# Loading four of an expert's 48 weight units as 112 + 8 + 8 rows instead of 128

## The chip, the cores and the metric

The kernel runs on one core of one Trainium2 chip. The time is device microseconds of one execution; before the change it is 1390.87 us as the median of three runs (1390.38 to 1391.24). TensorE (PE) multiplies, VectorE (DVE), ScalarE (ACT) and GpSimd (POOL) do the rest, SyncE (SP) does nothing but issue loads, and 16 transfer engines carry what is loaded.

## The reference

The reference is a trunk of two layers over 272 tokens (16 meta tokens and 256 frames) of width 1024, in float32. Each layer has an attention part and a feed-forward part; the first feed-forward part is dense, the second has eight experts of which each token uses two:

```python
def moe_swiglu(h, router_w, w_gate, w_up, w_down):
    logits = (h @ router_w).astype(jnp.float32)
    top_val, top_idx = lax.top_k(logits, TOP_K)
    gates = jax.nn.softmax(top_val, axis=-1)
    ...
    for e in range(N_EXPERTS):
        out = out + gate_dense[..., e:e + 1] * swiglu(h, w_gate[e], w_up[e], w_down[e])
    return out
```

with `swiglu(h, ...) = (silu(h @ w_gate) * (h @ w_up)) @ w_down` and an inner width of 3584. The expert weights alone are 352 MB, and every one of them is used once.

## The kernel before

**Stages.** Attention, dense feed-forward, attention, and then the expert stage, from about 522 us of the trace to its end. All weights lie in one HBM tensor, `stream`, cut into units of 128 rows (one row to a partition of the on-chip memory) by up to 2048 columns.

**An expert.** `moe_order` (lines 122 to 131) cuts it into 48 units: 32 of kind "w" (gate and up weights, 128 x 1792, 896 KB), then 16 of kind "d" (down weights; in each of four groups three of 128 x 2048, 1024 KB, and one of 128 x 1024, 512 KB). Every expert takes up to 96 tokens in three tiles of 32, one expert (the second in order of work) in two. For a "w" unit PE runs 12 matmuls (24 records of the trace), for a "d" unit 12 or 24; the second expert needs two thirds of that.

**The ring.** Unit m goes to slot m % 16 of `MOE_SLOTS` = 16 slots. Some slots lie in `moe_ring`, some in `parts_ring`, one in `sq`; those are three names for memory that earlier stages used. Each slot has its own semaphore, `slot_in[m % 16]`. A load adds 16 to it when it has landed, and PE waits for the count in `arrival` (line 990) before it reads the unit.

**Who sets the order.** SP runs `load_expert` (line 429 on) once per expert. For each unit it waits until PE is done with the unit 16 earlier (`w_used`), then issues one load of all 128 rows:

```python
sp.wait_ge(w_used, it * EXPERT_UNITS + (MOE_SPLIT + m - MOE_SLOTS + 1))
sp.dma_start(moe_unit(m), stream[e * EXPERT_UNITS + (MOE_AT + m), :, 0:moe_cols(key)]).then_inc(
    slot_in[m % MOE_SLOTS], 16)
```

The first expert is written out; the other seven run in a loop, so that SP's counts come out of registers. PE writes out the first six experts, and has register counts for the last two. POOL gathers the tokens of the next expert and adds up the results of the last one with DMAs of its own, which share the 16 transfer engines with the weights.

Of the kernel before, what the change touches and what calls it, by code (L numbers as in the profile page):

```python
# [41 lines left out]
P = 128  # L42
# [22 lines left out]
SLOTS = 6  # L65
HSLOTS = 3
MOE_SLOTS = SLOTS + 2 * HSLOTS + 4
# [8 lines left out]
MOE_AT = 2 * ATTN_UNITS + FFN_UNITS  # L76
# [3 lines left out]
EXPERT_UNITS = FF_GROUPS * (DK + (FF_TILES + 1) // 2)  # L80
# [39 lines left out]
def ffn_order():  # L120

    order = [("g", 0), ("u", 0)]
    for c in range(1, CHUNKS):
        order += [("g", c), ("u", c), ("d", c - 1)]
    return order + [("d", CHUNKS - 1)]


def moe_order():

    def up(g):  # L130
        return [("w", g, k) for k in range(DK)]

    def down(g):
        return [("d", g, i) for i in range((FF_TILES + 1) // 2)]

    return up(0) + up(1) + up(2) + up(3) + down(0) + down(1) + down(2) + down(3)


FFN_ORDER = ffn_order()
FFN_POS = {key: n for n, key in enumerate(FFN_ORDER)}  # L140
MOE_ORDER = moe_order()
MOE_POS = {key: m for m, key in enumerate(MOE_ORDER)}
# [2 lines left out]
def moe_cols(key):  # L145

    return 8 * FQ if key[0] == "w" else D * min(2, FF_TILES - 2 * key[2])


def is_direct(n):  # L150

    return (n - (ATTN1_AT if n >= ATTN1_AT else 0)) in DIRECT
# [14 lines left out]
def build(nc, stream, h0, gains, router_w, fnorm, consts, out):  # L167
    with ExitStack() as ctx:
        def sb(name, shape, dt=F32):
            return ctx.enter_context(nc.sbuf_tensor(name, shape, dt))  # L170

        def sem(name):
            return ctx.enter_context(nc.semaphore(name))
# [41 lines left out]
        key, least, smallest = sb("key", [P, EXPERTS]), sb("least", [P, EXPERTS]), sb("smallest", [P, 4])  # L215
# [75 lines left out]
        slot_in = [sem(f"slot_in{i}") for i in range(MOE_SLOTS)]  # L291
# [65 lines left out]
        def moe_unit(m):  # L357

            return moe_slots[m % MOE_SLOTS][:, 0:moe_cols(MOE_ORDER[m])]

        def moe_arrivals(m):

            return 16 * ((MOE_AT // SLOTS if m % MOE_SLOTS < SLOTS else 0) + m // MOE_SLOTS + 1)

        def arrived(eng, unit):

# [2 lines left out]
        def split(eng, unit):  # L369

            n = SPLIT_OF[unit]
            eng.wait_ge(split_lo, n + 1)
            return w_hi[:, n % HSLOTS, :], w_lo[:, n % HSLOTS, :]
# [8 lines left out]
        def o_(name, layer):  # L382
            return layer * N_OUTS + OUTS.index(name)
# [23 lines left out]
        @block.sync  # L407
        def _(sp):
            def load(n, cols=UNIT):
                if n >= SLOTS:  # L410
                    old = n - SLOTS
                    if is_direct(old):
                        sp.wait_ge(direct_used, DIRECT_OF[old] + 1)
                    else:
                        sp.wait_ge(split_lo, SPLIT_OF[old] + 1)
                sp.dma_start(ring[:, n % SLOTS, 0:cols], stream[n, :, 0:cols]).then_inc(slot_in[n % SLOTS], 16)

            for u, c, i, end in PIECES:
                sp.dma_start(ring[:, u, c], stream[u, :, c]).then_inc(slot_in[u] if end else first_in[i], 16)
            load(2)  # L420
            load(3)
            sp.dma_start(c_sb[:, :], consts).then_inc(const_in, 16)
            sp.dma_start(rw_sb[:, :, :], router_w).then_inc(rw_in, 16)
            for n in range(4, MOE_AT):
                b = n - ATTN1_AT if n >= ATTN1_AT else n
                load(n, used_cols.get(b, UNIT) if b < ATTN_UNITS else UNIT)
                if n == ATTN1_AT + U_T2:
                    sp.wait_ge(rope_done, 2 * N_ROPES)
                    sp.dma_start(gain_row, fnorm[:, 1, :]).then_inc(gain_in, 16)

            def load_expert(it, e):
                for m, key in enumerate(MOE_ORDER):
                    if m < SLOTS:
                        old = MOE_AT - SLOTS + m
                        if is_direct(old):
                            sp.wait_ge(direct_used, DIRECT_OF[old] + 1)
                        else:
                            sp.wait_ge(split_lo, SPLIT_OF[old] + 1)
                    elif m == 6:
                        sp.wait_ge(out_done, o_("g3", 1) + 1)  # L440
                    elif m in (7, 8):
                        sp.wait_ge(w_used, MOE_SPLIT - 2)
                    elif m in (9, 10):
                        sp.wait_ge(w_used, MOE_SPLIT - 1)
                    elif m == 11:
                        sp.wait_ge(mla_read, 2)
                    elif m in (12, 13, 14):
                        sp.wait_ge(w_used, MOE_SPLIT)
                    elif m == 15:
                        sp.wait_ge(tok_square, 4)  # L450
                    sp.wait_ge(w_used, it * EXPERT_UNITS + (MOE_SPLIT + m - MOE_SLOTS + 1))  # L451
                    sp.dma_start(moe_unit(m), stream[e * EXPERT_UNITS + (MOE_AT + m), :, 0:moe_cols(key)]).then_inc(  # L452
                        slot_in[m % MOE_SLOTS], 16)

            def load_others(r):
                with sp.Fori(1, EXPERTS) as n:
                    load_expert(r * EXPERTS + n, sp.value_load(order_sb[0:1, n, :], min_val=1, max_val=EXPERTS - 1))

            load_expert(0, 0)
            sp.wait_ge(order_ready, 1)  # L460
            load_others(0)
            sp.wait_ge(rounds_ready, 1)
            rounds = sp.value_load(rounds_sb[0:1, 0:1], min_val=1, max_val=ROUNDS)
            with sp.If(rounds > 1):
                with sp.Fori(1, rounds) as r:
                    load_expert(r * EXPERTS, 0)
                    load_others(r)
            with sp.Else():
                sp.nop()

            sp.wait_ge(res_ready, 1)
            sp.dma_start(out[0:P, :], res[:, 0, :]).then_inc(out_stored, 16)
            sp.wait_ge(res_ready, 2)
            sp.dma_start(out[P:2 * P, 0:512], res[:, 1, 0:512]).then_inc(out_stored, 16)
            sp.wait_ge(out_stored, 48)
# [138 lines left out]
        def _(pe):  # L614
# [310 lines left out]
            def dense():  # L925
                def gate_up(c):
                    for j, kind in enumerate("gu"):
                        w = [x.rearrange("p (k c) -> p k c", k=DK) for x in split(pe, DENSE_AT + FFN_POS[kind, c])]
                        first = c == 0 and j == 0
# [16 lines left out]
                def down(c):  # L946
                    w = [x.rearrange("p (f n) -> p f n", f=2) for x in split(pe, DENSE_AT + FFN_POS["d", c])]
                    pe.wait_ge(a_ready, c + 1)
                    if c == 0:
                        pe.wait_ge(std_ready, 2)  # L950
                    for d in range(DK):
                        if c or d >= 4:
                            pe.wait_ge(h_added, 8 + c * DK + d - 3)
                        for f in range(2):
                            mm3(bank[4 + d % 4][:, 0:L], [x[:, f, d * P:(d + 1) * P] for x in w],
                                [ad_hi[c % 2][:, f, :], ad_lo[c % 2][:, f, :]], f == 0, f == 1, d_done if f == 1 else None)
                    used_up.append((w_used, 1))
# [30 lines left out]
            def expert(it, last=False, tiles=range(TILES_OF), first=False):  # L988

                def arrival(key):  # L990

                    m = MOE_POS[key]
                    pe.wait_ge(slot_in[m % MOE_SLOTS], it * (16 * EXPERT_UNITS // MOE_SLOTS) + moe_arrivals(m))
                    return moe_unit(m)

                def both(s):
# [97 lines left out]
        def _(act):  # L1094
# [182 lines left out]
            def dense():  # L1277
                for m, (kind, c) in enumerate(FFN_ORDER):
                    n = SPLIT_OF[DENSE_AT] + m + HSLOTS
                    if kind == "u":  # L1280
                        act.wait_ge(af_ready, c + 1)
                        A(ad_hi[c % 2], a_dense, ACT.Copy).then_inc(a_hi_ready, 1)
                    if m < FFN_UNITS - 1:
                        high(n)
                    if kind == "g":
                        act.wait_ge(g_scaled, c + 1)
                        A(sil_dense, sil_dense, ACT.Silu).then_inc(silu_done, 1)
# [120 lines left out]
        def _(dve):  # L1408
# [242 lines left out]
            def dense():  # L1651
# [6 lines left out]

                for m, (kind, c) in enumerate(FFN_ORDER):
                    n = SPLIT_OF[DENSE_AT] + m + HSLOTS  # L1660
# [294 lines left out]
```

## Time and profile before

| | |
|---|---|
| median of three runs | 1390.87 us |
| the profiled execution, its own time | 1388.64 us |
| its span in the trace | 1386.8 us |
| granted TensorE clock, mean | 0.998 |
| PE busy | 1354.0 us, 98% |
| DVE, ACT, POOL busy | 469.0, 342.9, 84.2 us |
| moved from HBM | 438.20 MB |

The page's slices are a fortieth of the span each, 34.7 us. "Busy" for PE is time with a matmul under way. The DMA share of a stretch is the mean busy share of the 16 transfer engines; it can read a little over 1, since neighbouring packets of an engine overlap. A stretch's GB/s counts all queues.

### The profile page before, as it was taken

The page shows a single profiled execution, that of the slowest core. Times are in us where ns is not written, and L with a number is a line of the kernel's source. Part 1 is how long each engine was busy: PE and PEld are TensorE (multiplying, and loading weights), DVE is VectorE, ACT ScalarE, POOL GpSimd, SP SyncE. Part 2 cuts the span into 40 slices and gives each one's busy share as a digit, 9 for nine tenths or more (in the row PEclk, how much of TensorE's full clock was granted, in tenths as well). Part 3 has the DMA queues.
Part 4 walks back from the last instruction along what each step waited for, and adds up shares of the span by engine and source line. Part 5 has one row for each costly group of instructions (what it writes and reads, how often), then busy time and mean ns, then how long its engine had stood idle before and what let it go on. Part 6 is the DMA issues. An engine that isn't in the chain of part 4 may idle for free.

```text
span 1386.8 us, 34063 instructions
## 1 busy us (share of the span) xinstructions
PE 1354.0 (98%) x15034; PEld 866.5 (62%) x15034; DVE 469.0 (34%) x822; ACT 342.9 (25%) x594; POOL 84.2 (6%) x113
## 2 busy tenths in 40 slices
PE   9999999999999999999879999999999999999997
PEld 8889999999998894464333353363353354344344
DVE  7777777766797651101101101100100100110011
ACT  7666533333386641001000000000000000000011
POOL 0000000000000015001010010001001001001000
PEclk9999999999999999999999999999999999999999
DMA  9316644444433189999999999999999999999993
GB/s 362 112 58 244 228 166 162 174 183 183 183 134 138 62 325 412 417 418 408 418 414 416 419 417 410 419 417 412 419 417 409 418 417 410 417 415 406 419 414 137
DMA packets 74249, 443.98 MB, mean 320 GB/s; under 512 B 10116, under 2 KB 12224, under 8 KB 52992
## 3 DMA queue, kind: packets, MB, share of 16 engines
q1 hardware_dynamic: 67824, 433.04, 77.3%
q0 software_dynamic: 5424, 7.45, 2.0%
q8 instruction: 118, 1.93, 0.6%
q10 hardware_dynamic: 864, 1.40, 0.3%
q14 instruction: 19, 0.16, 0.0%
HBM read 438.20 MB, written 5.93 MB: 320 GB/s over the span
## 4 chain that ended last, share of the span: by engine, by line
PE 66%; SPq 19%; DMA 8%; DVE 2%; issue 2%; ACT 2%; ACTq 0%; DVEq 0%
PE bank L626 64%; SPq L452 19%; DMA moe_ring<-stream 6%; DMA parts_ring<-stream 2%; DMA hT<-h 1%; DVE w_lo L1425 1%; PE bank L630 0%; PE bank L724 0%; SPq L451 0%; DVE nmx L1510 0%; ACT scratch L1180 0%; PE bank L730 0%; ACT w_hi L1102 0%; ACT scratch L1179 0%; PE bank L1069 0%
## 5 line engine op out<-in xcount | busy, mean ns | idle before, releaser
L626 PE MATMUL bank<-parts,w_hi 128*128 128x272 f32 (+1 forms) x2240 | 427.5, 289 | 2.0 <-DVE parts L1439 1.7
L626 PE MATMUL bank<-moe_ring,hT 128*32 128x448 f32 x4416 | 425.3, 539 | 3.6 <-DMA moe_ring<-stream 2.9
L626 PEld LDWEIGHTS bank<-parts,w_hi 128*128 128x128 f32 x2240 | 351.9, 188 | 5.6 <-issue 4.2
L626 PE MATMUL bank<-parts,w_lo 128*128 128x272 f32 (+1 forms) x1120 | 321.4, 287 | 0.0
L626 PEld LDWEIGHTS bank<-moe_ring,hT 128*32 128x32 f32 x4416 | 149.3, 110 | 268.0 <-issue 242.0
L1777 DVE SCALAR_TENSOR_TENSOR hT<-bank,slot_norm,scratch 128x224 f32<-128x224 f32 x96 | 40.8, 425 | 727.3 <-ACT scratch L1332 727.2
L626 PE MATMUL bank<-moe_ring,scratch 128*32 128x256 f32 x4048 | 225.0, 379 | 9.3 <-DMA moe_ring<-stream 9.2
L626 PEld LDWEIGHTS bank<-parts,w_lo 128*128 128x128 f32 x1120 | 211.0, 188 | 0.2
L626 PEld LDWEIGHTS bank<-moe_ring,scratch 128*32 128x32 f32 x4048 | 133.9, 110 | 98.8 <-DMA moe_ring<-stream 16.1
L1332 ACT ACTIVATE scratch<-bank,norm_now 128x224 f32<-128x224 f32 x96 | 42.4, 447 | 513.6 <-PE bank L626 513.0
L1425 DVE TENSOR_TENSOR w_lo<-ring,w_hi 128x2048 fp32r<-128x2048 f32 x68 | 154.6, 2287 | 32.2 <-ACT w_hi L1102 32.1
L1102 ACT ACTIVATE w_hi<-ring 128x2048 fp32r<-128x2048 f32 x68 | 129.6, 1912 | 90.1 <-PE bank L626 90.0
L626 PE MATMUL bank<-parts_ring,hT 128*32 128x448 f32 x1104 | 112.9, 539 | 1.6 <-DMA parts_ring<-stream 1.6
L626 PEld LDWEIGHTS bank<-parts_ring,hT 128*32 128x32 f32 x1104 | 37.0, 110 | 69.0 <-issue 59.4
L1342 ACT ACTIVATE scratch<-bank,slot_gate 128x256 f32<-128x256 f32 x21 | 9.3, 474 | 246.3 <-PE bank L626 246.3
L1657 DVE TENSOR_TENSOR hT<-hT,bank 128x272 f32<-128x272 f32 x112 | 48.6, 435 | 20.8 <-PE bank L626 19.8
L626 PE MATMUL bank<-parts_ring,scratch 128*32 128x256 f32 x920 | 54.2, 379 | 1.1 <-DMA parts_ring<-stream 1.1
L576 POOL DMA_INDIRECT scratch<-hn_rows,row_of x24 | 25.0, 1040 | 448.5 <-DVE hT L1789 442.8
L585 POOL DMA_INDIRECT acc_rows<-scratch,row_of x21 | 33.3, 1587 | 213.4 <-ACT scratch L1342 209.1
L626 PEld LDWEIGHTS bank<-parts_ring,scratch 128*32 128x32 f32 x920 | 30.5, 110 | 20.7 <-DMA parts_ring<-stream 2.3
L1780 DVE STREAM_TRANSPOSE scratch<-hT 128x224 f32<-128x224 f32 x96 | 39.5, 411 | 3.3
L626 PE MATMUL bank<-sq,hT 128*32 128x448 f32 x368 | 37.6, 539 | 0.5 <-DMA sq<-stream 0.5
(227 smaller groups left out, 626.6 us busy)
## 6 DMA issues: line engine op xcount, KB each, us to landing
moe_ring<-stream SPq DMA_DIRECT2D x192, 896.0 KB, 24.1
moe_ring<-stream SPq DMA_DIRECT2D x80, 1024.0 KB, 25.3
ring<-stream SPq DMA_DIRECT2D x68, 1024.0 KB, 5.0
parts_ring<-stream SPq DMA_DIRECT2D x48, 896.0 KB, 23.8
parts_ring<-stream SPq DMA_DIRECT2D x16, 1024.0 KB, 24.9
sq<-stream SPq DMA_DIRECT2D x16, 896.0 KB, 23.6
moe_ring<-stream SPq DMA_DIRECT2D x16, 512.0 KB, 24.7
parts_ring<-stream SPq DMA_DIRECT2D x8, 512.0 KB, 25.1
```

What stands on the lines that cost most here:

```text
L452: sp.dma_start(moe_unit(m), stream[e * EXPERT_UNITS + (MOE_AT + m), :, 0:moe_cols(key)]).then_inc(slot_in[m % MOE_SLOTS], 16)
L576: pool.indirect_dma_start(out=x_rows[:, s, :], out_offset=None, in_=hn_quarters, in_offset=bass.IndirectOffsetOnAxis(ap=row_of[:, s, n:n + ...
L585: pool.indirect_dma_start(out=acc_quarters, out_offset=bass.IndirectOffsetOnAxis(ap=row_of[:, s, n:n + 1], axis=0), in_=ye[:, s, :], in_of ...
L626: return release(nc.tensor.matmul(dst, lhsT, rhs, start=start, stop=stop), inc, count)
L1102: A(w_hi[:, n % HSLOTS, :], slot(UNIT_OF[n]), ACT.Copy).then_inc(split_hi, 1)
L1332: A(sil_moe[:, s, :], bank[UP_BANKS[g][s]][:, 0:FQ], ACT.Silu, scale=norm_now[:, s:s + 1]).then_inc(e_silu, 1)
L1342: A(ye[:, s, :], bank[DOWN_BANKS[s]][:, 0:256], ACT.Copy, scale=slot_gate[:, it, s:s + 1]).then_inc(ye_ready, 1)
L1425: V.tensor_tensor(w_lo[:, n % HSLOTS, :], slot(UNIT_OF[n]), w_hi[:, n % HSLOTS, :].bitcast(F32), ALU.subtract).then_inc(split_lo, 1)
L1657: V.tensor_tensor(hT[:, d, :], hT[:, d, :], bank[4 + d % 4][:, 0:L], ALU.add).then_inc(h_added, 1)
L1777: V.scalar_tensor_tensor(out=a_moe[:, s, :], in0=bank[UP_BANKS[g][s]][:, FQ:2 * FQ], scalar=slot_norm[:, it, s:s + 1], in1=sil_moe[:, s, : ...
L1780: V.transpose(ht[:, g, s, :], a_moe[:, s, :]).then_inc(ht_ready, 1)
```

## The change

Units 5, 17, 29 and 41 of each expert ("w", "w", "w" and a "d" unit of 2048 columns) are loaded in three transfers: rows 0 to 111, 112 to 119 and 120 to 127. The rows, the memory they go to and the bytes are the same. All three add 16 to the slot's semaphore, so PE's count for such a slot is the sum of what its loads add.

```diff
+LEANING = (5, 17, 29, 41)
+LEAN_CUTS = (0, 112, 120, 128)
...
+        def moe_loads(m):
+
+            return len(LEAN_CUTS) - 1 if m in LEANING else 1
+
         def moe_arrivals(m):
 
-            return 16 * ((MOE_AT // SLOTS if m % MOE_SLOTS < SLOTS else 0) + m // MOE_SLOTS + 1)
+            each = [x for x in range(EXPERT_UNITS) if x % MOE_SLOTS == m % MOE_SLOTS]
+            count = (MOE_AT // SLOTS if m % MOE_SLOTS < SLOTS else 0) + sum(moe_loads(x) for x in each if x <= m)
+            return 16 * count, 16 * sum(moe_loads(x) for x in each)
...
-                    sp.dma_start(moe_unit(m), stream[e * EXPERT_UNITS + (MOE_AT + m), :, 0:moe_cols(key)]).then_inc(
-                        slot_in[m % MOE_SLOTS], 16)
+                    cuts = LEAN_CUTS if m in LEANING else (0, P)
+                    for a, b in zip(cuts, cuts[1:]):
+                        sp.dma_start(moe_unit(m)[a:b, :], stream[e * EXPERT_UNITS + (MOE_AT + m), a:b, 0:moe_cols(key)]).then_inc(
+                            slot_in[m % MOE_SLOTS], 16)
...
-                    pe.wait_ge(slot_in[m % MOE_SLOTS], it * (16 * EXPERT_UNITS // MOE_SLOTS) + moe_arrivals(m))
+                    count, each = moe_arrivals(m)
+                    pe.wait_ge(slot_in[m % MOE_SLOTS], it * each + count)
```

Rows that go 8 to an engine in a transfer of 128 go 7 to an engine in one of 112 spread over 16 engines; a transfer of 8 rows gives one row each to eight engines.

On SP, where the first expert's loads begin (`ring` is the memory of the stages before; each row is a run of equal loads), before:

```order
L416 DMA ring<-stream 128x2048 x4
L452 DMA moe_ring<-stream 128x1792 x6
L452 DMA parts_ring<-stream 128x1792
L452 DMA moe_ring<-stream 128x1792 x4
L452 DMA parts_ring<-stream 128x1792
L452 DMA moe_ring<-stream 128x1792 x2
```

and now:

```order
L424 DMA ring<-stream 128x2048 x4
L462 DMA moe_ring<-stream 128x1792 x5
L462 DMA moe_ring<-stream 112x1792
L462 DMA moe_ring<-stream 8x1792 x2
L462 DMA parts_ring<-stream 128x1792
L462 DMA moe_ring<-stream 128x1792 x4
```

The sixth load has become three, directly behind one another; nothing else changes its place.

On PE, where the loop over the last experts but one begins (`hT` holds the gathered tokens), before:

```order
L1088 ISA
L993 ISA
L626 MATMUL bank<-moe_ring,hT 32x448 x72
L993 REGISTER_ALU
L626 MATMUL bank<-parts_ring,hT 32x448 x12
```

and now:

```order
L1099 ISA
L1004 ISA
L636 MATMUL bank<-moe_ring,hT 32x448 x12
L1004 ISA
L636 MATMUL bank<-moe_ring,hT 32x448 x48
L1004 REGISTER_ALU
L636 MATMUL bank<-moe_ring,hT 32x448 x12
L1004 REGISTER_ALU
L636 MATMUL bank<-parts_ring,hT 32x448 x12
```

Slots no longer share one count per expert, so PE works out more register values between the same matmuls: 32 rows more in all (2642 after 2610).

## Rows read from the trace of the kernel before

**Rows 1.** The page's head, and its slices of the span.

```profile
span 1386.8 us, 34063 instructions
PE 1354.0 (98%) x15034; PEld 866.5 (62%) x15034; DVE 469.0 (34%) x822; ACT 342.9 (25%) x594; POOL 84.2 (6%) x113
...
GB/s 362 112 58 244 228 166 162 174 183 183 183 134 138 62 325 412 417 418 408 418 414 416 419 417 410 419 417 412 419 417 409 418 417 410 417 415 406 419 414 137
```

**Rows 2.** Busy time by stretch, one expert each from the second on.

```profile
core 0: us, PE busy (x) PEld busy (x) DVE busy (x) ACT busy (x) POOL busy (x), PEclk, DMA share, GB/s
630.40:717.80 87.40, 75.85 (x975) 32.89 (x964) 10.38 (x27) 6.41 (x18) 7.92 (x6) 1.00 1.02 414
717.80:827.90 110.10, 108.81 (x1438) 46.82 (x1436) 10.42 (x27) 6.75 (x18) 7.85 (x6) 1.00 1.02 416
827.90:936.40 108.50, 108.50 (x1447) 46.65 (x1440) 10.41 (x27) 6.89 (x18) 7.86 (x6) 1.00 1.02 415
936.40:1045.60 109.20, 108.75 (x1448) 46.34 (x1440) 10.41 (x27) 6.88 (x17) 7.88 (x6) 1.00 1.02 416
1045.60:1154.20 108.60, 108.60 (x1448) 46.67 (x1442) 10.42 (x27) 6.93 (x18) 7.84 (x6) 1.00 1.02 415
1154.20:1263.60 109.40, 108.65 (x1448) 46.63 (x1440) 11.93 (x33) 6.92 (x18) 7.92 (x6) 1.00 1.02 414
1263.60:1377.00 113.40, 112.08 (x1503) 49.24 (x1492) 11.99 (x26) 9.12 (x21) 5.57 (x4) 1.00 0.87 355
```

**Rows 3.** The DMA issues of SP's line 452: duration of an issue in ns.

```profile
L452 SPq DMA_DIRECT2D moe_ring<-stream x288: 327/1652/7537, 481.4 to 1343.2; - x144
L452 SPq MOVE moe_ring<-stream x252: 29/29/38, 597.6 to 1343.2; - x126
```

**Rows 4.** From the same view: time from issue to landing.

```profile
DMA to landing us min/median/max: 4.6/24.3/29.8
```

**Rows 5.** DMA issues by line, KB each, median us to landing.

```profile
moe_ring<-stream SPq DMA_DIRECT2D x192, 896.0 KB, 24.1
...
slot_sb<-slot_rows POOLq DMA_DIRECT2D x4, 28.1 KB, 5.6
```

**Rows 6.** PE in order of time, 1290 to 1300 us.

```profile
1290.60 2.46 PE L626 MATMUL bank<-parts_ring,hT 128*32 128x448 f32 x24 [1.12 <-DMA parts_ring<-stream]
1292.88 4.69 PE L626 MATMUL bank<-moe_ring,hT 128*32 128x448 f32 x48
1297.39 2.44 PE L626 MATMUL bank<-parts_ring,hT 128*32 128x448 f32 x24
```

**Rows 7.** Stretches about four 32-row loads of POOL (columns as in rows 2).

```profile
536.00:543.00 7.00, 7.00 (x80) 2.98 (x76) 2.35 (x6) 1.34 (x3) 2.32 (x4) 1.00 1.02 420
543.00:547.00 4.00, 4.00 (x48) 1.69 (x44) 0.00 (x0) 0.00 (x0) 0.00 (x0) 1.00 1.03 371
547.00:552.00 5.00, 5.00 (x60) 2.09 (x55) 0.00 (x0) 0.00 (x0) 3.17 (x8) 1.00 1.01 415
```

**Rows 8.** POOL after those loads.

```profile
547.66 0.28 POOL L560 CAST row_f<-slot_sb 128x75 f32<-128x75 int32 x1 [5.56 <-DMA slot_sb<-slot_rows]
```

**Rows 9.** Stretches at the head of the stage (columns as in rows 2).

```profile
500.00:510.00 10.00, 10.00 (x89) 10.00 (x88) 4.48 (x7) 1.90 (x5) 0.69 (x2) 1.00 0.71 262
510.00:520.00 10.00, 9.27 (x78) 8.69 (x77) 4.87 (x21) 4.33 (x12) 3.53 (x11) 1.00 1.01 410
```

**Rows 10.** DMA queues from 480 to 1377 us: packets, MB, share of 16 engines.

```profile
q1 hardware_dynamic: 55440, 353.39, 95.7%
q0 software_dynamic: 5120, 6.37, 2.7%
q8 instruction: 90, 1.47, 0.7%
```

## What the change was predicted to do

> **What bounds the kernel now.** I read the page's head first, to see where the loads run flat out: from the sixteenth slice on the stream stays at 406 to 419 GB/s, and before that it is mostly far below [rows 1]. The change touches only expert loads, so the question is what bounds that stretch. Cut by expert, the DMA share is 1.02 in every window from 630 to 1264 us: no transfer engine has time to spare there [rows 2]. PE is busy 108.5 us of 108.5 in one expert and 75.85 of 87.40 in the second one, which has only two tiles. PE's idle time is the window less its busy time: 11.55, 1.29, 0, 0.45, 0, 0.75 and 1.32 us, 15.4 us in all. That is all that a better stream could give back.
>
> PE and the stream are nearly equal. PE takes 2.28 us for a "w" unit (1290.60 to 1292.88) and 2.26 when nothing waits (4.51 for two) [rows 6]. A "w" unit is 896 KB, 917.5 kB, which at 415 GB/s is 2.21 us. PE's own pace thus has 0.05 us a unit over the stream, and a late landing stops PE as in the 1.12 us of [rows 6]. From issue to landing it takes 24 us as the median, about eleven units, and an issue itself takes 1.65 us against 0.33 at best [rows 3, 4]: SP stands in a full queue. So more issues cost SP nothing while that queue is full, and what counts is when the slowest of the 16 engines has its share done.
>
> **The change part by part.** In a full transfer each engine carries 8 rows, so a row of a "w" unit takes 2.21 / 8 = 0.275 us of an engine.
>
> *The row moved.* In a leaned unit one half of the engines has 7 rows and the other 9. If the half with 7 is the one that lands last, it is 0.275 us earlier per leaned unit. Of the 32 leaned units, the first lies about 500 to 510 us, where the share is 0.71 and the queue runs empty [rows 9]; what is saved there is lost again. Behind it the queue stays full, so 31 count: -8.5 us for that half, and +8.5 us for the other.
>
> *The cost of the form.* The trace has no transfer of 8 or of 112 rows. The nearest are POOL's four loads of 32 rows, 28.1 KB each [rows 5], which end before 547.66 us [rows 8]. While they run, the total falls from 420 to 371 GB/s, though the share is 1.03 [rows 7]: the engines are busy and move less. In these 4 us that is 196 kB less in total; the narrow loads are 115 kB of what is moved, so the weights lose 311 kB for 115 kB of narrow load, 2.7 for one. The two pieces of 8 rows are 16 x 7168 bytes = 115 kB as well. At 2.7 for one they take 311 kB of the stream instead of their own 115: 196 kB at 415 GB/s, 0.47 us a leaned unit. The bounds: nothing, if the narrow loads are slow only because their rows are short; and, from above, all 128 rows at 2.7 for one, 1.7 x 2.21 = 3.8 us. I take 0.47, since the 8-row pieces are what resembles that row; the 112-row piece I take as free. The net is 0.47 - 0.275 = +0.2 us for the half that lands last, and 31 x 0.2 = +6 us; the bounds are -8.5 (cut to -6 by what PE can give back, below) and 31 x 3.5 = +109 us.
>
> *Issues.* 64 more at 0.33 us are 21 us on SP if nothing hid them. SP has 2.2 us a unit and needs 0.33; three issues are 1 us. They are hidden by the full queue: 0.
>
> *Register work.* PE has 32 rows more; the nearest duration is a MOVE of 29 ns on SP [rows 3], 0.9 us if uncovered. PE's sequencer runs ahead of matmuls that are back to back: 0. The wait on 48 instead of 16 ends with the last piece, which is directly behind the others in the queue.
>
> The sum is made on the profiled execution: 1388.64 + 6 = 1394.6 us, of which 1.8 lie outside the span of 1386.8. The runs' median is 2.2 above the profiled time, so 1396.8, say 1397 us.
>
> At this place the Trainium skill weighs against the change. "SBUF — State Buffer", section "Door 1: The DMA port swizzle", says that the 128 partitions share 16 write ports, eight partitions to a port, four neighbours together, and that bandwidth goes by how many ports a transfer reaches. "DMA: Bandwidth & Descriptors", section "Why a DMA increments its semaphore by 16 and not by 1", says that a transfer of 8 rows runs on the eight lowest engines. By the two, eight engines push 8 rows through two ports that others are using. The trace agrees in direction, with its 371 after 420 GB/s, but its rows cannot tell ports from short packets. No view names an engine.
>
> **The rivals.**
>
> *Favourable: the form is free.* For it: rows of 7168 bytes are long, those of the narrow loads were short, and PE does wait for a stream whose mean rate would do. Something must make some engines later than others: instruction packets take 0.7% of 16 engines' 897 us, 100 us [rows 10]. If they all fall on eight engines, those are behind by 100 / 8 = 12.5 us at the end. The half with 7 rows gains 8.5, and the other half, 12.5 ahead, loses 8.5 and ends 4 ahead of where the late one was: 4 us gained at least, 6 if the gap is wider. From PE's side: by 727 us eight units are leaned, 2.2 us off the 11.55 idle, and the later idle 3.8 us go, 6 us. I take -5: 1386 us. Against it: it needs the misfit to be below 0.27 us, 4% of three transfers.
>
> *Pile-up.* Four neighbouring rows of an 8-row piece share one way into memory that passes a row in 0.275 us. The engine that always uses that way gets four strange rows for the one it is spared: +3 x 0.275 = +0.82 us a unit, 31 x 0.82 = +25, 1416 us; and if the 112 rows misfit likewise, up to 1500. It decides once a way carries no more than one engine does, since the share has no slack [rows 2]. Against it: a stream whose halves are many us apart may dodge it. By the page's ports this is the outcome; the trace does not show it.
>
> *The wrong half.* If the engines that take 9 rows are those that land last, then 31 x 0.275 = +8.5 us, 1399 us. Nothing in the rows says which half is late.
>
> *It does nothing.* If the engines' queues take the rows as before, whatever the shape, or gain and cost cancel: 1391 us.
>
> **How the numbers follow.** The forecast (a misfit near the narrow loads' price) has 0.34, favourable 0.33, pile-up 0.17, wrong half 0.06, nothing 0.10. The likeliest is the forecast by a hair, and its own range is 1393 to 1405. Within 0.2% is 2.8 us, about what a measurement of this kernel can tell from no change. Faster 0.34 takes the favourable case and the little of "nothing" that falls there; same 0.12 takes the rest of "nothing" and a forecast whose net comes out near 0; slower 0.54 is what remains. The range leaves out the upper part of the pile-up and the edge of the favourable: 1384 to 1440 us.
>
> **What would show it.** Right: the DMA share stays at 1.02 while GB/s in windows with a leaned unit is lower; an expert takes 0.8 us longer than 108.5 and PE waits for a load in every one. Favourable: GB/s unchanged or up, PE's idle time in the second expert's window falls by about 2 us and the later ones' is gone. Pile-up: an expert takes 3 us or more longer, and loads behind a leaned unit land later too, 27 us or more after issue. The form costs nothing at SP if its issues still have a median near 1.65 us. I am wrong in the net if experts come at 108.3 us with no waits, and wrong about SP if PE waits where SP's queue is short of loads.

## The result, and the profile after

| | before | after |
|---|---|---|
| median of the timed runs | 1390.93 us (4 runs) | 1569.87 us (4 runs, 1565.74 to 1587.72) |
| ratio after / before | | 1.1313, 95% interval 1.1285 to 1.1342 |
| the profiled execution, its own time | 1388.64 us | 1571.56 us |

The kernel is 13% slower. The forecast of 1397 us is wrong, and so is its range, which ended at 1440. The sign and the place were right, and the size was far off: 179 us over 32 leaned units are 5.6 us each, more than the 2.21 us that a whole "w" unit takes on the stream.

The page of the changed kernel, beside [rows 1]: its head, the DMA share and GB/s of the 40 slices (39.2 us each), the weights' queue, and the chain of waits by engine.

```profile
span 1569.7 us, 34255 instructions
PE 1399.4 (89%) x15034; PEld 854.6 (54%) x15034; DVE 469.2 (30%) x822; ACT 342.5 (22%) x594; POOL 84.1 (5%) x113
...
DMA  8334544454335999999999999999999999999993
GB/s 339 130 125 189 203 182 162 162 186 157 120 125 200 377 366 369 327 340 348 354 329 312 314 330 343 333 347 327 331 350 349 347 337 353 352 335 359 339 349 115
...
q1 hardware_dynamic: 68336, 433.05, 79.0%
...
PE 39%; SPq 38%; DMA 15%; issue 3%; DVE 2%; ACT 1%; ACTq 0%; DVEq 0%
```

The work is the same (PE has as many matmuls as in [rows 1]), and the engines of the transfers are as full as before. What they move has fallen from 406 to 419 GB/s to 312 to 377. In the chain, SP's full queue and the DMAs together (53%) now stand ahead of PE (39%). Before, the same line of the page read:

```profile
PE 66%; SPq 19%; DMA 8%; DVE 2%; issue 2%; ACT 2%; ACTq 0%; DVEq 0%
```

The windows by expert, columns as in [rows 2]:

```profile
631.50:757.00 125.50, 86.98 (x975) 31.58 (x965) 10.39 (x27) 6.42 (x18) 7.92 (x6) 0.93 1.02 347
757.00:901.80 144.80, 114.76 (x1440) 44.03 (x1436) 10.42 (x27) 6.74 (x18) 7.84 (x6) 0.99 1.02 320
901.80:1038.20 136.40, 114.32 (x1448) 43.40 (x1440) 10.42 (x27) 6.88 (x17) 7.86 (x6) 1.00 1.00 333
1038.20:1171.00 132.80, 114.62 (x1448) 44.82 (x1443) 10.41 (x27) 6.90 (x17) 7.87 (x6) 0.99 1.00 339
1171.00:1300.40 129.40, 113.15 (x1448) 45.27 (x1444) 10.42 (x27) 6.90 (x17) 7.83 (x6) 1.00 1.00 349
1300.40:1429.80 129.40, 112.70 (x1448) 44.27 (x1444) 11.93 (x33) 6.91 (x18) 7.92 (x6) 1.00 0.99 343
1429.80:1560.00 130.20, 119.15 (x1504) 48.25 (x1492) 12.01 (x26) 9.14 (x21) 5.57 (x4) 0.96 0.85 298
```

An expert of three tiles takes 129 to 145 us in place of 109. In the third to seventh expert of [rows 2] PE's idle time was 0 to 1.3 us each; it is now 16 to 30 us (144.80 less 114.76 is 30.0). The stage went from being bound by PE and the stream together to being bound by the stream alone. In the second expert's window PE's granted clock is 0.93, but PE stands idle for 38.5 us of it, so the clock is not what makes it longer. Every expert from the second on pays, so it is no mishap at one place. The first pays almost nothing yet: it takes 109.0 us (522.5 to 631.5) for 107.9, though its stream moves 362 GB/s for 415. PE is still fed there from what was loaded ahead, and the bill comes in the second expert, 38 us longer.

The loads into `moe_ring`, first what SP does, then who waits for them and how long from issue to landing, beside [rows 3] and [rows 4]; and PE's waits over the expert stage (us in all, times, longest):

```profile
L462 SPq DMA_DIRECT2D moe_ring<-stream x352: 242/1752/10242, 481.5 to 1525.8; - x176
...
DMA to landing us min/median/max: 10.2/28.5/35.5
```

```profile
PE bank L636 <- DMA moe_ring<-stream: 127.6, 123, 2.8
...
PEld bank L636 <- DMA moe_ring<-stream: 246.0, 200, 3.3
```

Before, PEld waited 38.7 us in 67 waits for `moe_ring`, and PE 12.0 us in 16. The longest of these waits has hardly grown, 3.3 us after 2.6: there is no long stop at the leaned units, PE is short of weights by a little at very many units. An issue has a median of 1.75 us for 1.65, so SP stands in a full queue as before, and the three issues are not what costs. A load lands 28.5 us after its issue instead of 24.3. The queue holds the same work, and the engines take longer for it.

That can be seen on single packets, which the trace keeps with their sizes and times (no view prints them). A row of a "w" unit is one packet of 7168 bytes. Before, its mean in the stage is 276 ns (half of them within 272 and 278); after, between 700 and 1500 us, it is 336 ns, a quarter take 360 or more, and one in twenty 536 or more, which is about twice 272. The rise, 1.22 times, is that from 340 to 415 GB/s. So it is not a few slow packets in the small pieces: the packets of the whole loads are longer too (those of the "d" units' 8192 bytes take 381 ns for 315), as would be seen if two engines took turns at one place.

The engines also drift apart in another way. Of one whole load of slot 15 these are the landings of its 16 shares, in us behind the first (one engine each):

```
before, at 1099.5 us:  0.6 3.5 3.5 4.0 4.1 4.2 4.4 | 11.8 12.4 12.7 13.5 13.6 13.8 14.1 16.0
after, at 1103.0 us:   0.2 0.2 0.3 0.3 1.0 1.0 1.4 2.4 2.8 5.0 6.5 6.6 13.8 17.9 20.7
```

Before there are two halves of eight. The means of the first eight and the last eight shares are 1 us apart at 531 us, 3 at 640, 10 at 1100 and 14 at 1317. This is the lean that the favourable rival supposed. After, the two halves are gone, and three engines are 14 to 21 us behind all others. A load is complete with its last share, so PE waits for the slowest engine.

### The profile page after: what moved, and what is told of

It is laid out like the page before. It is cut to its first block, busy times and chain, and to the rows that moved or that the text cites. A ratio compares the mean times of both kernels' runs of the same rounds, so it can differ in the third digit from the quotient of the medians.

```text
span 1569.7 us, 34255 instructions
## 1 busy us (share of the span) xinstructions
PE 1399.4 (89%) x15034; PEld 854.6 (54%) x15034; DVE 469.2 (30%) x822; ACT 342.5 (22%) x594; POOL 84.1 (5%) x113
## 4 chain that ended last, share of the span: by engine, by line
PE 39%; SPq 38%; DMA 15%; issue 3%; DVE 2%; ACT 1%; ACTq 0%; DVEq 0%
PE bank L636 38%; SPq L462 38%; DMA moe_ring<-stream 13%; DMA parts_ring<-stream 2%; DMA hT<-h 1%; DVE w_lo L1436 1%; SPq L459 0%; PE bank L640 0%; PE bank L734 0%; DVE nmx L1521 0%; ACT scratch L1191 0%; PE bank L740 0%; ACT w_hi L1113 0%; ACT scratch L1190 0%; PE bank L1080 0%
## 5 line engine op out<-in xcount | busy, mean ns | idle before, releaser
L636 PE MATMUL bank<-moe_ring,hT 128*32 128x448 f32 x4416 | 447.2, 548 | 82.5 <-DMA moe_ring<-stream 81.5
L636 PEld LDWEIGHTS bank<-moe_ring,hT 128*32 128x32 f32 x4416 | 140.4, 110 | 381.9 <-issue 202.0
L636 PE MATMUL bank<-moe_ring,scratch 128*32 128x256 f32 x4048 | 236.9, 385 | 46.5 <-DMA moe_ring<-stream 46.1
L636 PEld LDWEIGHTS bank<-parts_ring,scratch 128*32 128x32 f32 x920 | 30.6, 112 | 29.1 <-DMA parts_ring<-stream 11.8
```

The source lines that it names most:

```text
L636: return release(nc.tensor.matmul(dst, lhsT, rhs, start=start, stop=stop), inc, count)
```

## The experiments

**Theories.** *Places* (1): engines and the rows that they write no longer fit together, so that two engines at a time want the same way into the on-chip memory. *Fixed costs* (2): each further transfer costs the engines something whatever its form. *The small pieces* (3): the 8-row transfers are slow by themselves, as the prediction held. *The lean* (4): one row more on the eight engines that are late. And within the first, whether it is the place that is written or the place that is read.

In the kernels of the expert stage `moe_cuts(m)` gives the rows and columns of unit m's transfers; a "-" line is the change itself, written in that form. The loads of units not named stay whole, and PE's counts follow the number of transfers.

### e1: three transfers of all 128 rows each

```diff
-            return [(slice(a, b), slice(0, cols)) for a, b in ((0, 112), (112, 120), (120, P))]
+            return [(slice(0, P), slice(a, b)) for a, b in ((0, cols - 256), (cols - 256, cols - 128), (cols - 128, cols))]
```

> The four units of each expert in three transfers again, but cut by columns: 128 rows of all but 256 columns, then twice 128 rows of 128 columns (512 bytes a row). Every transfer keeps 8 rows to an engine. Theory 1 (ways into memory: the time comes from rows that an engine writes where another engine usually writes): no such row here, so 1391 to 1397 us, with GB/s of an expert window back at 410 or more. Rival (number of transfers, or the sum on one semaphore, costs): as the changed kernel, near 1570 us, since there are as many transfers.

Measured: 1393.74 us (1393.35 to 1394.46), ratio 1.0037 (1.0022 to 1.0051). The page's GB/s slices:

```profile
GB/s 362 109 58 245 230 166 166 166 179 182 182 151 134 61 328 408 417 414 407 416 408 417 417 414 408 417 415 409 416 415 407 416 401 410 410 410 406 417 405 158
```

The same number of transfers and issues in the same units, cut by columns, costs 5.0 us instead of 179, and the stream keeps its 401 to 417 GB/s. So the number of transfers, SP's issues and PE's register work are not the cause. The 5.0 us are 0.08 us for each of the 64 further transfers. They agree with the packets: a row is now 6144 + 512 + 512 bytes, 238 + 28 + 28 = 294 ns in place of 276; 18 ns by 8 rows by 32 units is 4.6 us.

### e2 and e3: two pieces, 112 + 16 and 64 + 64 rows

```diff
-            return [(slice(a, b), slice(0, cols)) for a, b in ((0, 112), (112, 120), (120, P))]
+            return [(slice(a, b), slice(0, cols)) for a, b in ((0, 112), (112, P))]   # e2
+            return [(slice(a, b), slice(0, cols)) for a, b in ((0, 64), (64, P))]     # e3
```

> The same units as 112 + 16 rows: two transfers, both over 16 engines, 7 and 1 rows to each, so no engine carries more than another. Theory 1 (ways into memory): the 112 rows stay where they were and are most of the bytes; between 1480 and 1600 us. Rival 1 (it is the lean: nine rows on eight engines): back to 1391 to 1400 us. Rival 2 (the eight-row pieces pile up on few ways and the 112 rows are harmless): 1420 to 1480, since 16 rows still come to the same places, by 16 engines.

> The same units as 64 + 64 rows: two transfers over 16 engines, 4 rows of each to an engine, no lean, no small piece. Theory 1 (ways into memory): all 16 engines write one half's eight ways at once, so a unit needs at least twice 2.21 us, and the other engines' units suffer too: 32 x 2.2 = 70 us or more over 1391, 1460 to 1600 us. Rival (small pieces or the lean): 1391 to 1397 us.

Measured: e2 1562.62 and 1592.67 us, too far apart for a ratio. No engine carries more than another there, and even the lower one is 174 us above the kernel before. e3 1573.99 us (1565.79 and 1582.19), ratio 1.1334 (1.1265 to 1.1402). The 100 us from 1000 on of e3 (columns as in rows 2):

```profile
1000.00:1100.00 100.00, 83.46 (x1114) 34.86 (x1108) 4.71 (x12) 4.22 (x11) 4.77 (x3) 1.00 0.99 344
```

With 64 + 64 there is no piece of 8 rows and nothing of 112, and the two pieces are alike, yet the price is the same within the runs' spread. So neither 8-row pieces nor a lean is needed for it: theory 3 is out as the cause, and theory 4 is at most a side matter. What the three row cuts share is that a unit's rows go out in a transfer that does not cover all 128.

### e4: one leaned unit per expert

```diff
-LEANING = (5, 17, 29, 41)
+LEANING = (17,)
```

> Only unit 17 of each expert in 112 + 8 + 8 rows, the other three whole. If every leaned unit has a price of its own (179 us / 32 = 5.6 us): 8 x 5.6 = 45 us less what PE's pace hides, 1420 to 1436 us. If the price is one of a state that the stream falls into and stays in: well over 1436. If one leaned unit is hidden by the queue and only several in a row hurt: under 1400.

Measured: 1443.24 us (1442.36 and 1444.12), ratio 1.0392 (1.0371 to 1.0413): 54.5 us for eight leaned units, 6.8 each. Its slices:

```profile
GB/s 361 119 59 236 234 175 176 176 173 174 121 124 136 174 380 408 417 389 385 417 406 358 418 409 336 418 409 329 419 415 329 412 416 356 377 409 386 358 409 109
```

That is above the 1420 to 1436 that I expected for a price of 5.6 us a unit. The stream falls to 329 to 358 once per expert and is back at 409 to 419 between. So a misfit heals within less than an expert, and each leaned unit pays its own price. Shorter stretches show how (columns as in rows 2, the first three around one leaned unit each):

```profile
646.00:656.00 10.00, 10.00 (x113) 4.07 (x106) 1.02 (x3) 1.20 (x3) 0.00 (x0) 1.00 1.00 237
868.00:888.00 20.00, 13.34 (x140) 3.68 (x132) 2.35 (x6) 1.34 (x3) 0.00 (x0) 1.00 1.02 269
1096.00:1124.00 28.00, 20.18 (x208) 5.69 (x204) 2.35 (x6) 1.34 (x3) 0.00 (x0) 1.00 1.02 305
1124.00:1136.00 12.00, 12.00 (x135) 4.13 (x130) 0.00 (x0) 0.00 (x0) 0.00 (x0) 1.00 1.01 418
```

One leaned unit, 2.2 us of stream by itself, slows the stream for 10, 20 and 28 us. Against 415 GB/s that is 4.3, 7.0 and 7.4 us lost. In the third a packet of 7168 bytes takes 380 ns in the mean, directly behind it (the fourth line) 277. The disturbance grows as the engines drift apart: the first and the last share of a load of slot 15 land 5 us apart at 643 us of e4, 14 at 866 and 21 at 1093, so it is 5 to 7 us longer than that distance each time. The further apart the engines are, the longer some of them are at the leaned unit while others are not. That this is the reason is my inference. In the changed kernel the next leaned unit comes twelve units or 26.5 us later, late in the stage before such a disturbance would be over. That may be part of why its price per unit is lower (5.6 us).

### e7: another place read, the same place written

```diff
+SHIFT = 36
...
-            return [(slice(a, b), slice(0, cols)) for a, b in ((0, 112), (112, 120), (120, P))]
+            return [(slice(0, P), slice(0, cols))]
...
+                        if m in LEANING:
+                            at = (MOE_AT + m) * P + SHIFT
+                            source = stream.rearrange("n p c -> (n p) c")[at:at + P, cols]
```

> Units 5, 17, 29 and 41 in one transfer of 128 rows as before, but its source begins 36 rows further on in HBM (and is the first expert's unit for every expert, so these weights are others). Each engine writes where it always writes and reads rows that another engine usually reads. Theory 1 (the price is paid where rows are written, in the on-chip memory): as before the change, 1387 to 1392 us. Rival (it is paid where rows are read, in HBM): tens of us more, up to 1570.

Measured: 1389.88 us (10 runs, 1389.49 to 1390.36), ratio 1.000 (0.9991 to 1.001).

```profile
1000.00:1100.00 100.00, 99.84 (x1347) 65.16 (x1343) 8.04 (x21) 5.56 (x14) 7.83 (x6) 1.00 1.02 415
```

In the same four units the rows read from HBM begin 36 rows further on, and what is written lies where it did. (They are always those of the first expert's unit, so this kernel leaves out the right weights of four units.) It costs nothing. For a transfer of 128 rows the place that is read does not matter, and I leave it out of the explanation.

### e8, e9 and e10: the same small transfer to three sets of places

All units are loaded whole. Behind each "w" unit goes one further transfer of 8 rows by 1 KB, into columns that no "w" unit uses. It has the same bytes and issues in the three kernels and takes the same part in the queue; only the partitions differ.

```diff
+LEANING = tuple(range(32))
...
+            return [(slice(0, P), slice(0, cols)), (slice(0, 32, 4), slice(cols, UNIT))]      # e8: rows 0, 4, .. 28
+            return [(slice(0, P), slice(0, cols)), (slice(64, 96, 4), slice(cols, UNIT))]     # e9: rows 64, 68, .. 92
+            return [(slice(0, P), slice(0, cols)), (slice(112, 120), slice(cols, UNIT))]      # e10: rows 112 to 119
```

> Nothing is split: each of the 32 'w' units is loaded whole, and a second transfer adds 8 rows of 1 KB (rows 0, 4, ..., 28, into columns that the unit leaves free; 256 such transfers). By theory 1 these eight rows go to eight different ways, which the eight engines that carry them use anyway. A row of 1 KB is about 0.04 us of an engine, 10 us in all for those eight engines. If they are the half that is ahead: 1389 to 1393 us. If they are the half that is late: 1398 to 1404.

> As the one with rows 0, 4, ..., 28, but with rows 64, 68, ..., 92: the same eight engines carry the same bytes, now to the eight ways that the other eight engines use. By theory 1 the other half is held up by what is written there, 0.04 us a unit or 10 us in all, and more if a held-up row costs more than its own length: 1398 to 1420 us, and above the run with the low rows by 8 us or more. Rival (only engines count, not places): the same time as the run with the low rows, within 3 us.

> As the two with every fourth row, but with rows 112 to 119, side by side. By theory 1 four of them share one way, so two ways get 4 x 0.04 = 0.16 us a unit, 256 x 0.16 = 41 us in all on the two engines that always write there: 1415 to 1440 us. Rival (only engines count): as the run with the low rows.

| | rows | us | ratio |
|---|---|---|---|
| e8 | 0, 4, .. 28 | 1407.87 | 1.013 (1.0113 to 1.0147) |
| e9 | 64, 68, .. 92 | 1416.37 | 1.019 (1.0173 to 1.0207) |
| e10 | 112 to 119 | 1420.83 | 1.0227 (1.021 to 1.0244) |

Only the places differ, and e9 is 8.5 us and e10 13.0 us above e8, with no overlap (the runs of each lie within 2 us). Both are where I expected them. 8.5 us over 256 transfers are 0.033 us each. This shows an effect of place on transfers of 8 rows, and in the order that theory 1 gave; but it is small.

My expectation for e8, 1389 to 1404, was missed. I had left out what such a transfer costs of itself: its packet of 1 KB takes 46 ns in the trace, 256 of them 11.8 us on an engine that has no slack. The other packets are longer too, 279.7 ns in e8, 283.4 in e9 and 281.5 in e10 for 276.4 before, which over 860 us is 10, 22 and 16 us. Together that is 22, 34 and 28 us for the 18, 27 and 31 that were lost. It does not explain why e10 is above e9; a mean over 16 engines does not say what the slowest did. Between 1000 and 1100 us the three move 405, 404 and 401 GB/s at a share of 1.00 to 1.01; the kernel before moves 415.

In e8 the two halves of a whole load have merged. At 1150.6 us its shares land at 0.0 0.1 ... 2.1 6.4 7.3 15.8 behind the first. That fits if the eight engines that took the small packets had been the early ones and lost their lead; one engine is 16 us late, and I have no cause for it.

### e5 and e6: only the 112 rows, only the 8-row pieces

From the second expert on (28 units) only a part of the four units is loaded.

```diff
+            return [(slice(0, P), slice(0, cols))] if first else [(slice(0, 112), slice(0, cols))]                        # e5
+            return [(slice(a, b), slice(0, cols)) for a, b in ((0, 64), (64, P))] if first else [(slice(a, b), slice(0, cols)) for a, b in ((112, 120), (120, P))]   # e6
```

> From the second expert on, units 5, 17, 29 and 41 bring only rows 0 to 111 (rows 112 to 127 keep what an earlier unit left there); the first expert's come whole. 28 leaned units, no eight-row piece. If the 112 rows carry the price, as 112 + 16 and 64 + 64 rows suggest: 28 x 4 to 5.6 us, less 28 x 0.28 us for the rows left out, 1490 to 1540 us. If the eight-row pieces carry it: 1383 to 1389.

> The other part alone: from the second expert on, these four units bring only rows 112 to 119 and 120 to 127 in two transfers (the first expert's come as 64 + 64 rows). That leaves out 28 x 1.93 us = 54 us of the stream, far more than the 15.4 us that PE can give back. If the eight-row pieces cost less than about 2 us a unit they are hidden, and the time is 1374 to 1390 us (the first expert's 64 + 64 rows may add up to 20). If they carry most of the 5.6 us: 28 x 3.7 = 103 us more than that, 1480.

Measured: e5 1529.98 us (1526.51 and 1533.45), ratio 1.102 (1.096 to 1.1079); e6 1395.78 us (1392.79 to 1396.16), ratio 1.0048 (1.0028 to 1.0067). Both from 1000 us on, e5 first:

```profile
1000.00:1100.00 100.00, 84.64 (x904) 28.46 (x900) 10.42 (x27) 6.91 (x17) 7.88 (x6) 0.97 1.02 334
```

```profile
1000.00:1100.00 100.00, 100.00 (x1356) 43.90 (x1352) 10.41 (x27) 6.91 (x17) 7.84 (x6) 1.00 1.02 397
```

The 112-row piece alone, with 475 kB less per expert to move, costs 141.6 us, 5.1 per unit. That is nearly the whole. It was the piece that I had taken as free.

In e6 PE has no idle time in this stretch, so what the 8-row pieces cost is hidden there by the 112 rows that are not loaded: 3326 kB an expert, 8.0 us at 415 GB/s, so at most about 2 us for each of four units. They are not free: the share is 1.02 although only 397 GB/s are moved. An estimate from this: 18 GB/s less than 415 over an expert's 109 us are 4.7 us, or 1.2 us for each of the four units. As to the 7.4 us above the kernel before, e6 loses them early. Counted by matmuls, PE is 0.5 us behind the kernel before when that one is at 613 us, 14 us behind at 703 us, and 7 at the end. So they come from the first expert's 64 + 64 rows or the first of the 8-row pieces; which of the two, this run does not say.

### e11 and e12: the price alone, on an idle queue

In the dense feed-forward stage the queue is not full (a whole unit of 1024 KB lands 5.0 us after its issue, in the expert stage 25.3). Twelve of its units of 1024 KB are cut, and the expert stage is left as before.

```diff
+CUT = tuple(range(DENSE_AT + 12, DENSE_AT + 36, 2))
...
-                sp.dma_start(ring[:, n % SLOTS, 0:cols], stream[n, :, 0:cols]).then_inc(slot_in[n % SLOTS], 16)
+                    sp.dma_start(ring[rows, n % SLOTS, c], stream[n, rows, c]).then_inc(slot_in[n % SLOTS], 16)   # e11: rows 0 to 111, 112 to 127; e12: columns 0 to 1791, 1792 to 2047
```

> The expert stage is as before. In the dense stage, where transfers often find an empty queue (a whole unit lands 5.0 us after its issue), twelve units are loaded as 112 + 16 rows. Theory 1: with nobody beside them, the engines of a 112-row transfer (896 KB) collide only with one another; it lands later than the same 896 KB by columns, by 0.5 to 2 us. If the price needs neighbours that are out of step: the same landing within 0.3 us. The whole time within 3 us of before, since this stage does not wait for the loads.

> The same twelve dense units as 128 rows of 1792 columns (896 KB) and 128 rows of 256 columns: the control for the run with 112 + 16 rows. The 896 KB transfers land 4.4 to 4.9 us after issue, a little less than the 5.0 of a whole unit; whole time within 3 us of before.

Measured: 1388.72 and 1389.07 us (8 runs each), ratios 1.0003 (0.9992 to 1.0015) and 1.0005 (0.9993 to 1.0016). The DMA issues of e11 and of e12 (KB each, median us from issue to landing):

```profile
ring<-stream SPq DMA_DIRECT2D x12, 896.0 KB, 6.1
...
ring<-stream SPq DMA_DIRECT2D x12, 128.0 KB, 6.9
```

```profile
ring<-stream SPq DMA_DIRECT2D x12, 896.0 KB, 4.5
...
ring<-stream SPq DMA_DIRECT2D x12, 128.0 KB, 4.6
```

Here the bytes of the pieces are equal. 896 KB as 112 rows land after 6.1 us, as 128 rows of fewer columns after 4.5: the misfit of such a transfer is 1.6 us where it runs beside little but its own small piece. The kernel's time does not show it, since nothing waits for these units. The same form costs 5 to 7 us per unit in the full stream, three to four times as much. There the loads around it are slowed as well, as e4's stretches of 10 to 28 us show.

**What the runs settle.** Cutting by rows costs, cutting by columns almost nothing (e1 against e2, e3); most of it sits in the large piece (e5 against e6); it belongs to each unit (e4) and is paid in longer packets of all loads around it. What they do not settle is why. The place read costs nothing in whole transfers (e7), and the place written matters for 8-row transfers, by 8.5 to 13 us in 256 of them (e8 to e10). No run writes the rows of a large piece to other places or by other engines. So the collision at a way into memory is an inference from these and from packets that take up to twice as long; no view shows such a way. That something else in how a transfer of 64 or 112 rows is dealt out to the engines lengthens the packets is left as a rival.

## Why the prediction was wrong

**The step that failed** is "the cost of the form", and in it the half sentence "the 112-row piece I take as free". The term was +0.47 us a unit, put on the two 8-row pieces. It measures 5.6 + 0.275 = 5.9 us if the row moved brought what I gave it, and e5 shows 5.1 of it in the 112 rows. My reason was that the 8-row pieces resembled the only narrow load in the trace [rows 5, 7]. Likeness of size was the wrong likeness: what the narrow loads showed was busy engines that move less. In those 4 us the weights' own packets of 7168 bytes took 310 ns in the mean, for 274 in the 7 us ahead of them, so the neighbours paid. This held for every transfer of fewer than 128 rows that I ran, and most for the one with seven times the rows of the two small pieces. The term for the small pieces was low as well, 0.47 us for an estimated 1.2 (e6).

**The upper bound was too low as well.** It took all 128 rows at 2.7 for one, 3.8 us. The 2.7 came from 4 us with four small transfers beside a stream, an extrapolation from 115 kB to eight times that. The measured price is (5.6 + 2.21) / 2.21 = 3.5 for one, and 4.1 where a leaned unit stands alone (e4). The range's end at 1440 then left most of even that bound out (+109 us is a time of 1500).

**The pile-up came nearest, and not in size.** It had 0.17, and its first number, 1416, put the price on the 8-row pieces at 0.82 us a unit; "up to 1500 if the 112 rows misfit likewise" was still 70 us short. Its sign posts came true: experts over 3 us longer (20 to 35 for three tiles), landings 27 us or more after issue (28.5). I weighed "a stream whose halves are many us apart may dodge it" against it; in e4 a leaned unit costs more, not less, late in the stage, where the engines are far apart. By the Trainium skill's page "SBUF — State Buffer", section "Door 1: The DMA port swizzle", bandwidth goes by the ports that a transfer reaches. By its table rows 0 to 63 reach 8 of the 16, and rows 0 to 111 all of them. I read it for the 8-row pieces, where the place makes 0.033 us a transfer (e9 against e8). For 64 + 64 rows the rule gives the right sign: I expected 2.2 us a unit or more (e3), and it measures 5.8. For the 112 rows by themselves, which reach every port, it gives nothing, and the measured price is 5.1 us (e5). So the ports that a transfer reaches do not price it here.

**The row moved.** The two halves exist, as the landings above show, at the end about as far apart (14 us) as the 12.5 us that I worked out from the instruction packets of [rows 10]. That the cause is those packets is not shown, so the agreement may be luck. The gain of 0.275 us a unit was never seen by itself: in all kernels that lean, the price is on top of it. It stays untested.

**Right.** The DMA share stays at 1.02 (1.00 to 1.02) while GB/s falls. SP's issues are hidden: their median is 1.75 after 1.65 us, and e1 has as many. The register work costs nothing that e1's 5.0 us, which the packets explain nearly whole, would leave room for. That PE had 15.4 us of idle time to give back did not matter in this direction: it had 0.05 us a unit to spare over the stream [rows 2, 6], so nearly every us of the stream became one of the kernel.

**Open.** Which rows each engine takes of 112, 64 or 16; why one engine of e8 and three of the changed kernel fall behind the rest; how the 7.4 us of e6 divide; why the price in the changed kernel falls from 35 us in the third expert to 20 in the seventh, while e4's rises. No kernel that I ran beats the one before: with row cuts the misfit is larger than any balance it could bring, and with column cuts the engines carry equal shares, which is no lean.

## What to carry to other kernels

In a stream whose transfer engines have no slack, keep every transfer at the full 128 partitions; where a load must be split, split it by columns (0.16 us a unit here, against 5.1 to 6.8 for a cut by rows). When the DMA share stays at 1 and GB/s falls, look at how many rows each transfer covers, before you count transfers or their issues. And when the form of the largest piece is one that the trace has never shown, that piece is the one to bound, from above by a multiple of itself, and not the one to call free.

## What the runs showed of the hardware that was not expected

- Two transfers of 64 rows cost as much as 112 + 8 + 8 (1.133 and 1.131 times), though each half of a unit is a large regular block.
- A misfit is worth three to four times as much in a full stream (5.1 to 6.8 us a unit) as alone (6.1 against 4.5 us to landing).
- One unit of 112 + 8 + 8 rows slows a full stream for 10 us at 646 us of the trace and for 28 us at 1096, and loses 4.3 and 7.4 us of it (e4).
- Shifting the rows that whole transfers read in HBM by 36 changes nothing (ratio 1.000, 0.9991 to 1.001).
- A transfer's rows cost by packet (SP's queue): 7168 bytes 276 ns, 6144 bytes 238, 1024 bytes 46, 512 bytes 28. From 512 to 7168 bytes that is about 9 ns a packet beside 0.037 ns a byte.
- In the kernel before, eight of the 16 engines fall behind the other eight, from 1 us at 531 us to 14 at 1317, without any lean in the loads. The instruction packets of [rows 10] take about 1.05 us each, so 90 of them on eight engines would be 12 us each. That they all fall on one half was not shown.
